# Expert rows of a two-layer encoder summed by 128x128 diagonal products, with the residual put into the sum banks

## What is computed

```
x = x + W_out( g_att * P_att(DiffAttn(n1(x))) + g_ssm * P_ssm(BiMamba2SSD(n1(x))) )
x = x + PEER(n2(x))

PEER, for a block of 128 tokens (hx), indices ix and gates gx of 128 experts per token:
    u = take(u_tab, ix)                                   # 128 tokens x 128 experts x 1024
    act = gelu(einsum('btkd,btd->btk', u, hx))
    wgt = act * gx
    return einsum('btk,btkd->btd', wgt, take(v_tab, ix))
```

## Time and profile before

| | us |
|---|---|
| runs shown | 2278.44, 2276.27, 2275.28 |
| median | 2276.27 |
| the profiled execution, its own time | 2278.7 |
| its span | 2276.9 |
| PE busy, 10000 matmul records | 1786.7 (78% of the span) |
| DVE busy | 1350.0 (59%) |
| ACT busy | 734.3 (32%) |
| POOL busy | 595.2 (26%) |
| L761, the products with the diagonals, 4096 records | 682 |
| indirect gathers, all queues | 59.2% of 16 DMA engines' span |

### The profile page before, as it was taken

How to read it: one execution, slowest core, us unless ns; L and a number is a source line. 1 busy time by engine, 2 the same in 40 slices (tenths; PEclk the granted TensorE clock), 3 DMA queues, 4 the chain that set the end, 5 groups by cost and what they waited for, 6 DMA issues and landing times.

```text
span 2276.9 us, 26598 instructions
## 1 busy us (share of the span) xinstructions
PE 1786.7 (78%) x10000; PEld 1092.9 (48%) x10000; DVE 1350.0 (59%) x3219; ACT 734.3 (32%) x2051; POOL 595.2 (26%) x598
## 2 busy tenths in 40 slices
PE   8999999998666655555599999999976667555555
PEld 7688888854322211111186888888533223111111
DVE  3377377158776576664525674761686766676644
ACT  2143365014333323322312434640243233232222
POOL 1000002024444343344210000110354444433432
PEclk9999999999987877778799999999988888777777
DMA  5433453779999999999943335547799999999996
GB/s 203 148 117 143 160 219 140 286 266 417 420 421 421 421 421 421 421 422 421 372 145 123 139 132 184 189 159 287 294 421 421 421 421 422 421 421 422 421 421 288
DMA packets 91473, 706.56 MB, mean 310 GB/s; under 512 B 10800, under 2 KB 10928, under 8 KB 16848
## 3 DMA queue, kind: packets, MB, share of 16 engines
q0 software_dynamic: 79424, 554.87, 59.2%
q1 hardware_dynamic: 11200, 146.33, 17.4%
q10 hardware_dynamic: 720, 3.67, 0.5%
HBM read 702.59 MB, written 1.18 MB: 309 GB/s over the span
## 4 chain that ended last, share of the span: by engine, by line
PE 50%; DMA 34%; DVE 7%; ACT 3%; POOL 2%; issue 2%; SPq 0%; POOLq 0%; DVEq 0%; ACTq 0%
PE bank L476 25%; DMA ring_c<-in_peer_uv,ex_i 12%; DMA ring_d<-in_peer_uv,ex_i 10%; DMA w_ring<-in_peer_uv,ex_i 7%; PE bank L761 7%; PE bank L459 5%; DMA ring_a<-in_peer_uv,ex_i 4%; PE bank L608 2%; PE bank L497 2%; PE bank L670 2%; DVE ring_c L1614 2%; PE bank L705 2%; DVE ring_d L1614 2%; ACT diag L1055 1%; DVE w_ring L1614 1%
## 5 line engine op out<-in xcount | busy, mean ns | idle before, releaser
L476 PE MATMUL bank<-hT,w_ring 128*128 128x256 f32 x2560 | 566.0, 381 | 0.8 <-DMA w_ring<-in_w_stream 0.8
L476 PEld LDWEIGHTS bank<-hT,w_ring 128*128 128x128 f32 x2560 | 483.8, 191 | 71.7 <-issue 6.6
L1043 ACT ACTIVATE gel<-act_u 128x2 f32<-128x2 f32 x260 | 52.8, 203 | 809.0 <-DVE ring_d L1614 169.6
L761 PE MATMUL bank<-ring_a,diag 64*64 64x512 f32 x832 | 139.9, 801 | 109.0 <-ACT diag L1055 109.0
L761 PE MATMUL bank<-w_ring,diag 64*64 64x512 f32 x832 | 144.5, 826 | 95.8 <-ACT diag L1055 95.8
L761 PE MATMUL bank<-ring_d,diag 64*64 64x512 f32 x832 | 134.3, 770 | 91.6 <-ACT diag L1055 91.3
L761 PE MATMUL bank<-ring_f,diag 64*64 64x512 f32 x800 | 131.1, 783 | 89.5 <-ACT diag L1055 89.3
L761 PE MATMUL bank<-ring_c,diag 64*64 64x512 f32 x800 | 132.3, 790 | 79.0 <-ACT diag L1055 79.0
L1756 POOL DMA_INDIRECT ring_a<-in_peer_uv,ex_i x104 | 103.3, 994 | 324.8 <-DVE ex_i L1534 165.2
L1614 DVE SCALAR_TENSOR_TENSOR ring_a<-ring_a,h 128x1024 f32<-128x1024 f32 x104 | 123.4, 1224 | 88.9 <-DMA ring_a<-in_peer_uv,ex_i 88.8
L1614 DVE SCALAR_TENSOR_TENSOR ring_d<-ring_d,h 128x1024 f32<-128x1024 f32 x104 | 123.5, 1223 | 87.7 <-DMA ring_d<-in_peer_uv,ex_i 87.6
(11 more groups left out here) (274 smaller groups left out, 2455.6 us busy)
## 6 DMA issues: line engine op xcount, KB each, us to landing
w_ring<-in_w_stream SPq DMA_DIRECT2D x60, 2048.0 KB, 8.3
fbuf<-cs_rows_dram POOLq DMA_DIRECT2D x32, 512.0 KB, 5.4
wq<-in_w_stream SPq DMA_DIRECT2D x6, 2048.0 KB, 12.8
out<-in_w_stream SPq DMA_DIRECT2D x2, 2048.0 KB, 15.1
keys<-in_keys_t ACTq DMA_DIRECT2D x2, 1024.0 KB, 5.0
ring_a<-in_peer_uv,ex_i POOLq DMA_INDIRECT x104, 15.1
w_ring<-in_peer_uv,ex_i POOLq DMA_INDIRECT x104, 14.6
ring_d<-in_peer_uv,ex_i POOLq DMA_INDIRECT x104, 15.2
```

The source lines that it names most:

```text
L476: ins = pe.matmul(two(m % 2)[:, j % 2, :], w[:, k, j * P:(j + 1) * P], hT[:, k, :], start=(k == 0), stop=(k == KD - 1))
L761: ins = pe.matmul(bank[b0 + half_of][n * HB:(n + 1) * HB, :], diag[tokens, PAIR * (m % 2) + s, :], ring[PLACE[m]][tokens, s, DM + n * 512: ...
L1043: act.activation(gel[:, b, c0:c1], act_u[:, b, c0:c1], ACT.Gelu).then_inc(gelu_done.sem, 1)
```

## The change

- The diagonals are 128x128: ACT scales the identity matrix, and the constant `blocks` and the size `HB` are gone. `diag` grows accordingly.
- PE multiplies all 128 tokens at once, 2 instructions of 128x128 by 512 per slot in place of 4 of 64x64 by 512. Feature half n of block b is summed in bank 4 + 2b + n.
- Ahead of each block PE puts the residual into the two banks, by two products of `x_tok[:, b, :]` with the identity, and the sums are added to it there.
- `take_block` copies instead of adding. Block 0 is copied by DVE in two instructions. Of block 1 DVE copies the first half of the features, and ACT the second (`take_shifted`), at the start of the next layer's norm or of the last one.

```diff
@@ -81,8 +81,7 @@
 NPAR = _at
 
 
-HB = P // 2
-CONST_SIZES = [("ident", P), ("tri_le", P), ("tri_ge", P), ("ones", P), ("blocks", HB), ("sign", 1), ("iota", TOPK), ("freq", 1)]
+CONST_SIZES = [("ident", P), ("tri_le", P), ("tri_ge", P), ("ones", P), ("sign", 1), ("iota", TOPK), ("freq", 1)]
 CONST = {}
 _at = 0
 for _n, _s in CONST_SIZES:
@@ -268,7 +267,7 @@
         act_u, at = place(at, "act_u", [P, TB, SLOTS])
         gel, at = place(at, "gel", [P, TB, SLOTS])
         wgt, at = place(at, "wgt", [P, TB, SLOTS])
-        diag, at = place(at, "diag", [P, 2 * PAIR, HB])
+        diag, at = place(at, "diag", [P, 2 * PAIR, P])
 
         bank = [ctx.enter_context(nc.psum_tensor(f"bank{i}", [P, 512], F32)) for i in range(8)]
 
@@ -299,6 +298,7 @@
         trig_step = once("trig_step")
         trig_ready = once("trig_ready")
         x_ready = sem("x_ready", TB)
+        x_shifted = sem("x_shifted", 1)
         alog_exp = sem("alog_exp", 1)
         sq_done = sem("sq_done", 4)
         ms_ready = sem("ms_ready", 4)
@@ -750,18 +750,18 @@
                 for b in range(TB):
                     b0 = 4 + 2 * b
                     pe.wait_ge(mix_empty.sem, mix_empty.at(L, 10 + 2 * b))
+                    for n in range(2):
+                        pe.matmul(bank[b0 + n][:], ident, x_tok[:, b, n * 512:(n + 1) * 512], start=True, stop=True,
+                                  skip_group_check=True)
                     for k in range(BLOCK_PAIRS):
                         m = BLOCK_PAIRS * b + k
                         for n_step, slots in pair_steps(m):
                             pe.wait_ge(diag_ready.sem, diag_ready.at(L, n_step))
                             for s in slots:
                                 for n in range(2):
-                                    for half_of in range(2):
-                                        tokens = slice(half_of * HB, (half_of + 1) * HB)
-                                        ins = pe.matmul(bank[b0 + half_of][n * HB:(n + 1) * HB, :],
-                                                        diag[tokens, PAIR * (m % 2) + s, :],
-                                                        ring[PLACE[m]][tokens, s, DM + n * 512:DM + (n + 1) * 512],
-                                                        start=(k == 0 and s == 0), stop=True, skip_group_check=True)
+                                    ins = pe.matmul(bank[b0 + n][:], diag[:, PAIR * (m % 2) + s, :],
+                                                    ring[PLACE[m]][:, s, DM + n * 512:DM + (n + 1) * 512],
+                                                    start=False, stop=True, skip_group_check=True)
                             ins.then_inc(pair_used.sem, 1)
                         if m == 0:
                             key_scores(2, 0)
@@ -802,6 +802,12 @@
                 wait(ms_ready, u + 1, L)
                 act.activation(rms[:, b0:b1], rms[:, b0:b1], ACT.Sqrt).then_inc(rms_ready.sem, 1)
 
+            def take_shifted(L):
+
+                act.wait_ge(pair_used.sem, pair_used.at(L, LAYER_STEPS))
+                act.activation(x_tok[:, 1, 512:DM], bank[7][:], ACT.Copy).then_inc(x_shifted.sem, 1)
+                wait(x_shifted, 1, L)
+
             def gained(m0, gain, L):
                 param = param_of(L)
                 cols = slice(0 if L == 0 else P, SEQ)
@@ -824,6 +830,7 @@
                     wait(ms_ready, 1, L)
                     act.activation(rms[:], rms[:], ACT.Sqrt).then_inc(rms_ready.sem, 1)
                 else:
+                    take_shifted(L - 1)
                     act.wait_ge(x_ready.sem, x_ready.at(L, 1))
                     squares(0, L, 1, TB)
                 if L == 0:
@@ -1052,7 +1059,7 @@
                         if m >= 2:
                             act.wait_ge(pair_used.sem, pair_used.at(L, m - 1))
                         for s in slots:
-                            ins = act.activation(diag[:, PAIR * (m % 2) + s, :], const("blocks"), ACT.Copy,
+                            ins = act.activation(diag[:, PAIR * (m % 2) + s, :], ident, ACT.Copy,
                                                  scale=wgt[:, b, j + s:j + s + 1])
                         ins.then_inc(diag_ready.sem, 1)
 
@@ -1104,6 +1111,7 @@
                             if m == tiles[3] + 2:
                                 scores_out(t0, qb)
 
+            take_shifted(DEPTH - 1)
             act.wait_ge(x_ready.sem, x_ready.at(DEPTH, 1))
             squares(0, DEPTH, 1, TB)
 
@@ -1620,11 +1628,8 @@
                 def take_block(b):
 
                     dve.wait_ge(pair_used.sem, pair_used.at(L, BLOCK_PAIRS if b == 0 else LAYER_STEPS))
-                    for half_of in range(2):
-                        tokens = slice(half_of * HB, (half_of + 1) * HB)
-                        for n in range(2):
-                            xs = x_tok[tokens, b, n * 512:(n + 1) * 512]
-                            ins = dve.tensor_tensor(xs, bank[4 + 2 * b + half_of][n * HB:(n + 1) * HB, :], xs, ALU.add)
+                    for n in range(TB - b):
+                        ins = dve.tensor_copy(x_tok[:, b, n * 512:(n + 1) * 512], bank[4 + 2 * b + n][:])
                     ins.then_inc(x_ready.sem, 1)
 
                 first_eight()
@@ -1785,7 +1790,6 @@
     c[:, col["tri_le"]] = i[:, None] <= i[None, :]
     c[:, col["tri_ge"]] = i[:, None] >= i[None, :]
     c[:, col["ones"]] = 1.0
-    c[:, col["blocks"]] = np.tile(np.eye(HB), (2, 1))
     half = ROPE // 2
     sign = np.ones(P, np.float32)
     freq = np.zeros(P, np.float32)
```

## The result

| | before | after |
|---|---|---|
| median of 6 runs each, us | 2277.14 | 2285.10 |
| lowest to highest | 2275.28 to 2278.90 | 2283.33 to 2286.38 |
| the profiled execution: its time, its span | 2278.7, 2276.9 | 2284.75, 2281.8 |

The changed kernel is slower: ratio 1.0032, 95% interval 1.0022 to 1.0043. The medians differ by 8.0 us, the two profiled spans by 4.9 us. The traces account for the 4.9. The forecast of 2277.5, no measurable change, was 7.6 us too low. That 2285.1 lies just inside the range is owed to the room that the range left for rival A, not to the forecast's own sum; the mechanism is that of rival A.

A forecast was written before the change was run, and what follows sets the result against it. The prediction took the gathers, at 421 GB/s of DMA, to bound the steady part. Layer ends -2.3, weights +0.6 and openings +3.0 gave +1.3 us on 2276.27: 2277.5 us, no measurable change, range 2271.5 to 2286.

The forecast's parts named there:

- rival A: Opening of each gather stage: the ring of gathered rows runs dry, 5 us more lost per layer, 2285.8 us; chance 0.22.
- Steady part, 0: Middle of the gather stages: PE's pairs 1.55 us longer, covered by the gather queue, full clock held; cost 0.
- Rival C: Steady part of the gather stages: PE stays cold, 6.9 us a pair, 245 us per layer, 2770 us; chance 0.02.
- Residual, 0: Ahead of each block: two identity products, 1.72 us, hidden in PE's gap or under the queue; cost 0.
- Turns of pairs 2 to 6: Opening: five PE turns without a gap, each 1.55 us longer, their ends late by 2.0 to 8.2 us.
- The opening, +1.5 per layer: Start of each gather stage: 0.6 us lost at pair 5 and 0.9 at two later edges, +3.0 in all.
- leads: Opening: gathers of pairs 8 to 12 and 14 to 16 issued 7.3 to 9.4 us ahead, called just enough.
- the need: Opening: time a gather requires, 4.98 us of transfer and 1 to 3 from issue to traffic, 6 to 8 us.
- The 0.6 us that it set for pair 5: Opening: pair 1 ends later and frees pair 5's place late, where DMA engines run short; 0.6 us lost per layer.
- End of layer, -1.15 per layer: Last row of each layer: diagonal +0.05, PE's row +0.9, copies on DVE and ACT -2.1 us; -2.3 in all.
- Weights of layer 1, +0.6: Start of layer 1: first weights sent later, behind longer pair 126, delaying the first product 0 to 1.5 us; +0.6 taken once.
- Sum: Whole kernel: ends -2.3, weights +0.6 and openings +3.0 make +1.3 us, a median of 2277.5 us.

The follow-up runs named there:

- e4: Kernel before with one extra 128x128 by 512 product per slot in pairs 40 to 55 of each layer; 2277.48 us, ratio 1.0004.
- e5: Changed kernel without the two identity products; DVE adds both banks to the residual and ACT copies nothing; 2290.66 us, ratio 1.0053.
- e12: e8 again, timed in one call with the kernel before and e11; 2273.36 us, ratio 0.9978.
- e9: Kernel before with one extra 128x128 by 512 product per slot in pairs 2 to 6 of each layer; 2289.40 us, ratio 1.0056.
- e2: Block 0 summed as in the changed kernel, block 1 as in the kernel before; 2287.53 us, ratio 1.0044 against the kernel before.
- e3: Kernel before with one extra 128x128 by 512 product per slot in pairs 0 to 15 of each layer; 2299.16 us, ratio 1.0097.
- e10: Kernel before with one extra 128x128 by 512 product per slot in pairs 7 to 15 of each layer; 2276.93 us, ratio 1.0004.
- e11: Kernel before with two identity products ahead of pair 0 of each layer, their result overwritten; 2276.20 us, ratio 0.9991.
- e6: Changed kernel with both copies of block 1 on DVE, one after the other; 2285.07 us, one execution.
- e7: Changed kernel with the router's first late tiles moved one pair later, behind pairs 2 to 5; 2289.87 us, ratio 1.0047 against the kernel before.
- e8: e1 with two identity products ahead of pair 0 of block 0, their result overwritten; 2273.94 us, ratio 0.9979 against the kernel before.
- e1: Block 0 summed as in the kernel before, block 1 as in the changed kernel; 2275.14 us, ratio 0.9992 against the kernel before.

## Where the prediction was right and where it was wrong, by its steps

- **Steady part, 0: right.** Pairs of 3.70 us with gaps of 1.28, clock 1.00, 422 GB/s; e4 says the same of added PE time. Rival C did not happen.
- **Residual, 0: right**, and more than that: e5 shows that without it the changed kernel would lose another 6.2 us of stage time over both layers. The gap of 2.33 us left pair 0 warm in both layers of the profiled run; e12 shows that it need not.
- **Turns of pairs 2 to 6: right.** Pair 6 late by 8.0 us (541.5 against 533.5; forecast 8.2), of which the five turns made 7.5.
- **The opening, +1.5 per layer: this step failed.** Measured are +4.1 in layer 0 (stage 655.7 against 651.6) and +2.8 in layer 1. Most leads were well worked out, but the need was not. The text set "6 to 8 us": 4.98 of transfer and 1 to 3 from issue to traffic. No pair found in an opening got along with so little. Pairs 0, with nothing ahead of them, took 8.1 us and more from the first gather instruction to the landing of the second row, though their second instruction comes 2.72 us behind the first; of the others the shortest found is 8.4 us (pair 8 in e9, at 525.42). Pair 5 of before, which the prediction used for its delay, took 9.1 (508.98 to 518.06). In layer 0 of the changed kernel the two pairs that lost time took 11.4 us (pair 8) and 11.9 (pair 15); the others from 7 to 16, 10.3 to 11.8, lost none. Pair 8 had a lead of 8.6 us (525.9 to 534.5): 2.8 lost. The prediction had 9.4 for it; it let the gather follow 0.48 us behind pair 3's end, where in before it came 0.88 behind (521.18 to 522.06) and now 0.93. It took leads of 7.3 us and more for enough. The 0.6 us that it set for pair 5 cost nothing in layer 0: pair 5 landed 1.6 us later than before (519.7 against 518.1), pair 7 not at all.
- **What adds to the need:** POOL sends a pair in two instructions one after the other, and the second starts only behind the first: 1.24 us later as a rule, 2.27 for pair 8, whose first instruction took 1.97 us instead of 0.94. That such instructions exist stood in the trace of before: 1.80 us at 523.30. There the queue covered it. Both began while DVE was at a dot product, and ended 0.82 us behind it (see the last section); for pair 8 it is this one:

```profile
525.83 1.22 DVE L1622 SCALAR_TENSOR_TENSOR ring_c<-ring_c,h 128x1024 f32<-128x1024 f32 x1
```

  The long instruction can place the loss, but it does not make it: e2, with the same block 0, sent pair 8 with instructions of 0.99 and 0.94 us, lost 1.4 us there and 2.4 more at pairs 11, 15 and 16, and its stage is as long, 655.8 us.
- **End of layer, -1.15 per layer: right in kind, too large.** It is -0.8 in both layers. The take gave 2.04 as forecast (2.1). The single row took 1.88 us instead of 1.09 (+0.8; forecast +0.9), and another 0.4 us came from something that the text had not: the last pairs are taken row by row, and PE runs the last four rows without a gap, each two in 3.60 us (two from 1132.92, two from 1136.35), so it begins the last row at 1138.07, where its diagonal was ready at 1137.60.
- **Weights of layer 1, +0.6: it was 0.** They are issued at 1136.61 instead of 1130.37 but the first product at 1144.73 waits for ACT's hT (0.15 us), not for them.
- **Sum.** 4.1 + 2.8 in the openings, -1.6 in the ends; the stage of layer 0 also started 0.3 us later, and the way from the last dots of layer 0 to the first gather of layer 1 was 0.6 us shorter beyond the shorter end: that way took 478.5 us in before and 477.9 to 478.3 in e3, e4, e9, e10 and e11, whose code there is the same, so this term is chance for the most part. 6.9 - 1.6 + 0.3 - 0.6 = 5.0, the 4.9 us of span but for rounding.
- **The chances.** Rival A, 0.22, at 2285.8, is what happened; its price of 5.6 us per layer is above the measured 4.1 and 2.8. Its "for" (shares of 0.74 and 0.88 already, DVE full) was a fact about the trace; its "against" rested on the lower end of an estimated need. Pair 5's own landing, 9.1 us after its issue with only pair 4 still under way, would have replaced the estimate by a measurement: against it pair 11's lead of 7.3 us is 1.8 short, the opening loses 2.4 us instead of 1.5, and the sum becomes 2279.4. That would have moved the forecast towards A, whose case begins at 3.2 us per layer, but not the whole way: the pairs that ran late here needed 11.4 and 11.9 us.

## What to carry to other kernels

When an engine's turn gets longer ahead of a queue, compare the lead of each transfer with the whole time that an unhindered transfer of the same kind took in the trace, from first issue to last landing, not with transfer time plus a guessed delay; and take even that for the least, since with others under way it was 2 to 3 us more here (9.1 against 11.4 and 11.9). A change that is free in the steady part can cost where the stage opens, since there turns follow one another without a gap and each delay is added to the next; try the new form in the other blocks alone, as here, where it gave the gain without the loss. Work of no use put into a wait kept the clock up here in most cases, and can pay only if what follows is short of time.

## What the runs showed of the hardware

- **A gather's latency.** Layer 0's first two gathers, one row of 1.05 MB each, nothing queued ahead of them, took 5.6 and 5.4 us from issue to landing (the tile ring_a of the changed kernel, at 479.7 and 482.4):

```profile
DMA to landing us min/median/max: 5.6/5.6/5.6
...
DMA to landing us min/median/max: 5.4/5.4/5.4
```

  At 421 GB/s the transfer of one row is 2.5 us, so some 3 us are not transfer. The Trainium skill (DMA: Bandwidth & Descriptors, Anatomy of one DMA — SWDGE (gpsimd) path) puts a fixed 2.0 us beside the bytes; by it a row would take 4.4 us, an estimate, and the rows measured here took a microsecond more.
- **A gather instruction on POOL waits for DVE's dot product.** It takes 0.94 us, or up to 2.00. Over the 14 traces 1536 of the 7168 began while DVE was in a dot product (L1614 before, L1622 after), and 1524 of these ended 0.82 us behind that dot's end, to within 0.05. So did 318 of 330 that began under a TENSOR_TENSOR of 128x512 of the router. Under MAX8 and FIND_INDEX8 one of 575 took over 1.1 us, and with DVE in no instruction two of 4195. All this is read from the order of events in the traces; no run moved a dot product to test it.
- **Two engines reading PSUM at once** do not slow each other down: 0.60 us on ACT and 0.69 on DVE, both from 1139.98 on, are the single prices of the earlier trace rows. The Trainium skill (PSUM — Partial Sum Buffer, Specifications) says so for different banks; the trace agrees.
- **The clock** stayed full in turns of 3.70 us with gaps of 1.28 us. Of the 14 pairs 0 behind gaps of 2.2 to 2.3 us (both layers of after, e2, e6, e7, e8, e11 and e12) eleven ran at 2.4 GHz throughout, and three at 1.2 GHz for at least a part: e7's layer 1 (5.40 us), e12's layer 0 (3.64) and e11's layer 1 (2.40). Behind gaps of 4.0 to 4.1 us all 14 pairs 0 (both layers of before, e1, e3, e4, e5, e9 and e10) were at 1.2 GHz for at least a part: their mean granted clock was 0.50 to 0.78.
